# One diffusion-backbone layer on one Trainium2 core: the first adaLN product taken in blocks of output channels, inside the first projection

## The reference, cut to what matters

```python
mod_x = (silu(c) @ w_ada + b_ada)          # 6 x 1024 values
mod_c = (silu(c_ctx) @ w_ada + b_ada)
sh1, sc1, g1, sh2, sc2, g2 = split(mod_x, 6)
csh1, csc1, ... = split(mod_c, 6)
hc = rms(ctx) * norm_pre_mix * (1 + csc1) + csh1
hx = rms(x) * norm_pre_mix * (1 + sc1) + sh1
k_c, v_c = hc @ w_in[:, K_OFF:G_OFF]       # context: keys and values only
proj = hx @ w_in                           # q, k, v, gate, Fourier part
```

## Time and profile before

| | us |
|---|---|
| median of 3 runs (lowest, highest) | 1516.63 (1514.66, 1517.1) |
| the profiled execution, its time | 1513.78 |
| its span, first to last instruction | 1511.9 |
| TensorE busy (share of the span) | 1493.0 (99%) |
| VectorE, ScalarE, GpSimd busy | 1255.2, 588.9, 427.7 |
| first pass of the first projection starts | 42.60 |

### The profile page before, as it was taken

One profiled execution on the slowest core, in us unless ns is written; L12 is line 12 of the kernel. 1 busy time (PEld: TensorE's weight loads), 2 busy tenths in 40 slices (PEclk: granted clock), 3 DMA queues, 4 the chain that ended last, 5 costly groups with the idle time before them and its releaser, 6 DMA issues.

```text
span 1511.9 us, 21849 instructions
## 1 busy us (share of the span) xinstructions
PE 1493.0 (99%) x8129; PEld 1314.1 (87%) x8129; DVE 1255.2 (83%) x2378; ACT 588.9 (39%) x877; POOL 427.7 (28%) x365
## 2 busy tenths in 40 slices
PE   9999999999999999999999999999999999999998
PEld 4788888788999999999999999988888888888887
DVE  6888748766899997899999955688888888888886
ACT  6433133622233333444444443343333333333333
POOL 1020000000368888533222211321322222222210
PEclk9999999999999999999999999999999999999999
DMA  9685113134248887889999999999999999999983
GB/s 389 218 291 175 56 57 100 54 84 154 91 171 280 282 296 264 276 314 357 386 360 370 366 341 348 377 410 379 371 354 375 378 370 380 382 369 371 365 320 130
DMA packets 148438, 431.39 MB, mean 285 GB/s; under 512 B 13328, under 2 KB 46352, under 8 KB 145424
## 3 DMA queue, kind: packets, MB, share of 16 engines
q1 hardware_dynamic: 73152, 203.91, 37.0%
q0 software_dynamic: 41472, 151.01, 27.4%
q10 hardware_dynamic: 33744, 75.64, 13.2%
HBM read 375.98 MB, written 54.53 MB: 285 GB/s over the span
## 4 chain that ended last, share of the span: by engine, by line
PE 85%; DVE 10%; POOL 2%; DMA 1%; ACT 1%; issue 1%; ACTq 0%; SPq 0%; DVEq 0%
PE ps L1711 26%; PE ps L1713 25%; PE ps L1712 25%; PE ps L2122 3%; POOL ws_lo L610 1%; PE ps L2062 1%; DVE ps L1540 1%; DVE rows L1508 1%; DMA ada_w<-w_ada 1%; DVE ps L1544 1%; POOL rows L618 1%; DVE picks L1546 1%; PE ps L1956 0%; PE ps L1944 0%; DMA g_dram<-g_buf 0%
## 5 line engine op out<-in xcount | busy, mean ns | idle before, releaser
L1711 PE MATMUL ps<-hT_hi,ws_hi 128*128 128x384 f32 (+1 forms) x1184 | 412.0, 348 | 5.4 <-POOL ws_lo L610 4.3
L1713 PE MATMUL ps<-hT_hi,ws_lo 128*128 128x384 f32 (+1 forms) x1184 | 405.4, 342 | 0.0
L1712 PE MATMUL ps<-hT_lo,ws_hi 128*128 128x384 f32 (+1 forms) x1184 | 405.1, 342 | 0.0
L1711 PE MATMUL ps<-vs_hi,coef_hi 128*128 128x512 f32 x768 | 299.3, 390 | 1.1 <-DVE coef_lo L1670 1.1
L1712 PE MATMUL ps<-vs_lo,coef_hi 128*128 128x512 f32 x768 | 299.1, 389 | 0.0
L1713 PE MATMUL ps<-vs_hi,coef_lo 128*128 128x512 f32 x768 | 299.1, 389 | 0.0
L912 ACT ACTIVATE ws_hi<-blk_raw 128x1024 fp32r<-128x1024 f32 x128 | 135.7, 1060 | 323.2 <-PE ps L1713 323.2
L966 ACT ACTIVATE vs_hi<-blk_raw 128x1024 fp32r<-128x1024 f32 x128 | 135.7, 1060 | 285.3 <-PE ps L1713 282.8
L1711 PEld LDWEIGHTS ps<-hT_hi,ws_hi 128*128 128x128 f32 x1184 | 222.6, 188 | 14.8 <-issue 4.8
L1713 PEld LDWEIGHTS ps<-hT_hi,ws_lo 128*128 128x128 f32 x1184 | 222.3, 188 | 6.3
L1712 PEld LDWEIGHTS ps<-hT_lo,ws_hi 128*128 128x128 f32 x1184 | 222.7, 188 | 5.5
(11 more groups left out here) (321 smaller groups left out, 1850.7 us busy)
## 6 DMA issues: line engine op xcount, KB each, us to landing
blk_raw<-u_t SPq DMA_DIRECT2D x128, 512.0 KB, 6.1
blk_raw<-v_nat SPq DMA_DIRECT2D x128, 512.0 KB, 7.4
g_dram<-g_buf ACTq DMA_DIRECT2D x128, 192.0 KB
w_dram<-w_stage SPq DMA_DIRECT2D x48, 512.0 KB, 8.6
grp_g<-g_dram ACTq DMA_DIRECT2D x15, 1536.0 KB, 9.8
grp_w<-w_dram ACTq DMA_DIRECT2D x15, 1536.0 KB, 25.5
part_w<-w_ada POOLq DMA_DIRECT2D x32, 512.0 KB, 6.1
raw<-w_in SPq DMA_DIRECT2D x20, 512.0 KB, 6.4
```

What stands on the lines that cost most here:

```text
L1711: pe.matmul(o, lh, rh, start=start, stop=False, skip_group_check=True)
L1712: pe.matmul(o, lh, rl, start=False, stop=False, skip_group_check=True)
L1713: return pe.matmul(o, ll, rh, start=False, stop=stop, skip_group_check=True)
```

## The change

The host lays columns 0 to 2047 of w_ada out anew (ada_mix): block kc holds, for 128 output channels, all 1024 input rows of their shift and their scale, 1 MB. On the chip:

- ada_products(kc) takes the block's 2 x 8 tiles of 128 x 128 as weights in full precision and the two silu vectors as two moving columns. The sums come out as columns, in four spare columns of bank 7 (bank 5 for kc = 1); no splitting, no rows, no small transposes. modulation(kc) is two small VectorE steps per block.
- TensorE's order: block 0, x's transposes for kc = 0, then the projection's piece 0, in which kc's products of x and ctx stand beside the transposes of later channels and, after two of the four x products, the adaLN block kc + 1. VectorE modulates straight from PSUM; the copies to xT and cxT are gone.
- SyncE loads x in four pieces, then block 0, unit 0, ctx, and blocks and units by turns; before unit 8 it waits for all transposes of x. GpSimd's first part load waits for block 5's product, its third for the last transposes of ctx.
- x's squares start with each piece; the ctx norm moves behind block 0 on both engines. WARM is 9, KEEP is gone.

Lines of the same kind are cut; a line "..." stands for what is left out.

```diff
-ADA_WHOLE = 2
-ADA_HALVES = 2
-WARM = 12
-KEEP = 2
+WARM = 9
...
-        ada_w = [at(f"ada_w{k}", rE + 8 * K * k if k < 4 else rF + 8 * K * (k - 4), [2 * D]) for k in range(KC)]
...
+        ada_at = (rF, rF + 8 * K, rG, rG + 8 * K, rJ, rI + 8 * K, rI, rH)
+        ada_w = [at(f"ada_w{kc}", ada_at[kc], [KC, 2, P]) for kc in range(KC)]
+        junk_x = at("junk_x", rA + 12 * K, [D])
+        part_w = [at(f"part_w{i}", (rI + 8 * K, rI + 12 * K, rJ + 8 * K, rJ + 12 * K)[i], [D]) for i in range(PART_RING)]
...
+        ada_sums = [ps[:, 5 if kc == 1 else 7, NCTX:NCTX + 4].rearrange("p (s t) -> p s t", s=2) for kc in range(KC)]
...
+            def load_ada(kc):
+                sp.dma_start(ada_w[kc][:], ada_mix[kc:kc + 1, :, :].rearrange("a p n -> p (a n)")).then_inc(ada_in[kc], 16)
+
+            for tb in range(TB):
+                sp.dma_start(xs[:, tb, :], x[tb * P:(tb + 1) * P, :]).then_inc(x_in[tb], 16)
+            load_ada(0)
+            load_unit(0)
             sp.dma_start(cx[:], ctxt.rearrange("(b p) d -> p b d", p=P)).then_inc(cx_in, 16)
-            for kc in range(KC):
-                sp.dma_start(ada_w[kc][:], w_ada[kc * P:(kc + 1) * P, 0:2 * D]).then_inc(ada_in[kc], 16)
-            for n in range(n_units):
+            for j in range(1, RAW):
+                load_ada(2 * j - 1)
+                load_ada(2 * j)
+                load_unit(j)
+            load_ada(KC - 1)
+            for n in range(RAW, n_units):
                 if n == 8:
 
+                    sp.wait_ge(tr_done, KC)
...
-            pool.wait_ge(tr_done, 2 * KC)
+            pool.wait_ge(ada_used, 6)
             for u in range(parts):
+                if u == 2:
+
+                    pool.wait_ge(ctr_done, KC)
...
-            def take_x(kc):
...
             round_unit(0)
-            act.wait_ge(ada_used, KC)
-            act.activation(mod_rows[0:4, 0:D], ps[0:4, 0:2, :].rearrange("p a n -> p (a n)"),
-                           ACT.Copy).then_inc(rows_out, 1)
-            act.wait_ge(ada_done, 1)
-            act.activation(mod_rows[0:4, D:3 * 512], ps[0:4, 2, :], ACT.Copy).then_inc(rows_out, 1)
+            round_column(0, False)
+            act.wait_ge(cx_in, 16)
+            square(cx[:, 0, :], TB, 2)
+            act.wait_ge(ms_done, 5)
+            act.activation(rs[:, TB:TB + CB], ss[:, TB:TB + CB], ACT.Sqrt).then_inc(rt_done, 1)
+            for kc in range(KC):
+                round_column(kc, True)
+                if kc + 1 < KC:
+                    round_column(kc + 1, False)
+                if kc % 2 == 0 and kc < KC - 2:
+                    round_unit(kc // 2 + 1)
...
-            for kc in range(4):
...
+            def modulation(kc):
+
+                dve.wait_ge(ada_used, kc + 1)
+                dve.tensor_tensor(mod_b[:, kc::KC, :], ada_sums[kc],
+                                  colp[:, C_BADA + kc:C_BADA + 2 * KC:KC].unsqueeze(2).broadcast_to([P, 2, 2]),
+                                  ALU.add).then_inc(mod_step, 1)
+                dve.wait_ge(mod_step, 2 * kc + 1)
+                dve.tensor_scalar(mod_a[:, kc, :], mod_b[:, KC + kc, :], 1.0, colp[:, C_NPM + kc:C_NPM + kc + 1], ALU.add,
+                                  ALU.mult).then_inc(mod_step, 1)
+                dve.wait_ge(mod_step, 2 * kc + 2)
+
+            def modulated(kc, context):
+                t, src = ((xT, ps[:, 6, :]), (cxT, ps[:, 7, 0:NCTX]))[context]
+                dve.wait_ge((tr_done, ctr_done)[context], kc + 1)
+                dve.tensor_scalar(t[:, kc, :], src, mod_a[:, kc, context:context + 1], mod_b[:, kc, context:context + 1],
+                                  ALU.mult, ALU.add).then_inc(full_done, 1)
...
-            for j in range(4):
...
+            modulation(0)
+            modulated(0, 0)
+            rest_unit(0)
+            modulated_rest(0, 0)
+            dve.wait_ge(cx_in, 16)
+            square(cx[:, 1, :], TB + 1, 3)
+            scaled(1, cx, TB, CB, 3, 4)
+            for kc in range(KC):
+                modulated(kc, 1)
+                modulated_rest(kc, 1)
+                if kc + 1 < KC:
+                    modulation(kc + 1)
+                    modulated(kc + 1, 0)
+                    modulated_rest(kc + 1, 0)
+                if kc % 2 == 0 and kc < KC - 2:
+                    rest_unit(kc // 2 + 1)
...
+            def ada_products(kc):
 
                 pe.wait_ge(ada_in[kc], 16)
-                for n in range(4):
-                    last = pe.matmul(ps[0:4, n, :], csil[:, kc, :], ada_w[kc][:, n * 512:(n + 1) * 512],
-                                     start=kc == 0, stop=False, skip_group_check=True)
+                if kc >= 2:
+
+                    pe.wait_ge(full_done, 2 * kc)
+                for s in range(2):
+                    for k in range(KC):
+                        last = pe.matmul(ada_sums[kc][:, s, :], ada_w[kc][:, k, s, :], csil[:, k, 0:2], start=k == 0,
+                                         stop=k == KC - 1, skip_group_check=True)
                 last.then_inc(ada_used, 1)
 
-            def ada_split(kc):
...
+            def transposed(kc, context):
+                if kc:
+                    pe.wait_ge(full_done, 2 * kc - 1 + 2 * context)
+                else:
+                    pe.wait_ge(xn_done, (TB, TB + CB)[context])
+                for tb in range(CB if context else TB):
+                    src = (cx if context else xs)[:, tb, kc * P:(kc + 1) * P]
+                    last = pe.transpose(ps[:, 6 + context, tb * P:(tb + 1) * P], src, ident[:])
+                last.then_inc((tr_done, ctr_done)[context], 1)
 
             pe.wait_ge(iotas, 2)
             keep_busy(WARM)
             pe.wait_ge(silu_done, 1)
-            ada_chunk(0)
+            ada_products(0)
             pe.wait_ge(ident_ld, 16)
-            for kc in range(4):
...
+            transposed(0, 0)
...
+                    def row_product(kc, r):
+                        th, tl, tb, bank = rows_of[r]
+                        return split_mm(ps[:, bank, :], th[:, kc, tb * P:(tb + 1) * P], tl[:, kc, tb * P:(tb + 1) * P],
+                                        hi[:, kc % 2, :], lo[:, kc % 2, :], kc == 0, kc == KC - 1)
+
+                    for kc in range(2 * j, 2 * j + 2) if p == 0 else ():
+                        if kc:
+                            transposed(kc, 1)
+                            if kc + 1 < KC:
+                                transposed(kc + 1, 0)
+                        pe.wait_ge(full_lo, 2 * kc + 1)
+                        for r in range(TB):
+                            if kc and r == 2 and kc + 1 < KC:
+                                ada_products(kc + 1)
+                            row_product(kc, r)
+                        if kc == 0:
+                            transposed(1, 0)
+                            ada_products(1)
+                            transposed(0, 1)
+                        pe.wait_ge(full_lo, 2 * kc + 2)
+                        for r in range(TB, TB + CB):
+                            if kc == 0 and r == TB + 1:
+                                pe.wait_ge(mod_step, 3)
+                            last = row_product(kc, r)
...
+    ada_mix = ada[:, 0:2 * D].reshape(KC, P, 2, KC, P).transpose(3, 1, 0, 2, 4).reshape(KC, P, 2 * D)
```

More of the change, by code:

```diff
@@ L643, in _, with square @@
                            ACT.Silu).then_inc(silu_done, 1)
[L644 to L652, removed]
-            act.activation(guard[:], csil[:, 0, 2:3], ACT.Sqrt)
-            act.wait_ge(x_in, 16)
-            squares([(xs[:, tb, :], tb) for tb in range(2)], 0)
+            act.activation(guard[:], csil[:, 0, 2:3], ACT.Sqrt)
+            def square(src, bank, done):
+                if done:
+                    act.wait_ge(sq_done, done)
+                act.activation(junk[:], src, ACT.Square, accum_out=ss[:, bank:bank + 1]).then_inc(sq_done, 1)
+            act.wait_ge(x_in[0], 16)
+            square(xs[:, 0, :], 0, 0)
+            act.wait_ge(x_in[2], 16)
+            square(xs[:, 2, :], 2, 1)
             act.wait_ge(ms_done, 3)
             act.activation(rs[:, 0:TB], ss[:, 0:TB], ACT.Sqrt).then_inc(rt_done, 1)
[L659 to L662, removed]
             def round_full(src, dst, m):
@@ L738, in _ @@
                         take_piece(p - 1)
-                    if p or j:
+                    if p:
                         round_unit(4 * p + j)
[L741 to L745, removed]
                 if 0 < p < n_proj - 1:
@@ L1021, in _, with square, scaled @@
         def _(dve):
[L1022 to L1034, removed]
+            dve.wait_ge(silu_done, 1)
+            def square(src, bank, done):
+                if done:
+                    dve.wait_ge(ms_done, done)
+                dve.tensor_tensor_reduce(junk_x[:], src, src, 1.0, 0.0, ALU.mult, ALU.add,
+                                         ss[:, bank:bank + 1]).then_inc(ms_done, 1)
+            def scaled(i, t, first, count, by_act, by_dve):
+                dve.wait_ge(sq_done, by_act)
```

(13 more changed lines are left out.)

150 lines of the change are left out of this document (28 added, 122 removed).

## The result

The changed kernel takes **1548.92 us** (median of 4 runs, 1545.48 to 1550.22) where the kernel before, on the same chip, takes 1515.89: a ratio of 1.0211, 95% interval 1.0199 to 1.0224. It is slower by 33 us. The forecast was 1540, with a range of 1528 to 1554. The profiled execution took 1545.48 us, 31.7 more in its span than the earlier trace rows.

What follows compares the result with a forecast made beforehand. TensorE, busy 99% of the span, was taken as the bound, with VectorE's feed. Projection 9.8, piece 1 3.3 and turn() 7.9 make 21.0; clock 2.6 makes 23.6 on 1513.78, 1537.4; median 2.85 above: 1540 us, range 1528 to 1554.

Steps and rivals of the forecast that it cites:

- the list: First projection: TensorE's adaLN work goes from 18.3 to 29 us, so the projection ends at 85.1, 9.8 us later.
- the lead: VectorE's 8.1 us lead at piece 1 is lost: TensorE stalls 3.3 us there and 7.9 at turn().
- rival (b): First projection: each block's two-column passes drop the clock, slowing following products, 14 us more, 1552 us; chance 0.10.
- turn term: At turn() TensorE waits for VectorE's up_lo: 7.9 us, bounds 0 to 13.
- the start of piece 1: After the first projection: 9.8 us later from the projection plus a 3.3 us stall for rest_unit(4).
- I take 1.3 for each, 2.6: Clock lost after 2.8 idle us before the first products and 7 at turn(): 2.6 us together, bounds 0 and 8.
- 4.1 of 8.55 us are dense: First projection, argument against rival (b): 4.1 us of each 8.55 us kc are dense products.
- VectorE's stretch: From rest_unit(4)'s start to the end of up_lo, VectorE needs 68.8 us, as before the change.
- rival (a): Before turn(): VectorE catches up as part loads arrive without waits, turn() costs 0 to 3 us, 1533 us; chance 0.17.
- (c): adaLN blocks: two-column passes nearly free, 256 passes save 28 of 29 us, 1510 us; chance 0.04.
- (d): adaLN blocks: at 0.02 to 0.03 us a pass, gain and lost lead cancel, no change, 1516 us; chance 0.03.
- Rival (e): First projection: VectorE paces each kc, 1 us a kc, 7 us more, 1547 us; chance 0.08.

Runs made afterwards that it cites:

- Wide: Changed kernel with the silu columns repeated 64 times, so each adaLN pass streams 128 columns instead of 2; 1536.23 us, ratio 1.0143.
- reordered: Wide with only the order changed: unit 4's rest before VectorE's first three parts; 1538.69 us, one run.
- few-products: Wide with one instead of eight 128-row tiles in each adaLN sum of blocks 1 to 7; 1513.97 us, one run.
- Wide and parts together: Wide with eight of 32 parts added during the first projection and add_parts(0) taken from ahead of rest_unit(4); 1525.26 us, ratio 1.0065.
- interleaved kernel: Changed kernel with each block's 32 passes in four groups of eight, one behind each of x's products; 1555.04 us, ratio 1.0257.
- no-lead kernel: Kernel before the change, with VectorE held from unit 4's rest until TensorE is through with piece 0; 1525.73 us, ratio 1.0074.

## Why the prediction was right or wrong

**Right: direction, range, and the two terms of the list and of the lead.** The point was 9 us too low, and the range held the result because it had been stretched to rival (b), which had a chance of 0.10; a turn term 2 us too large hid a little of the miss. Wide tests the two terms without the clock of thin passes. First product 18.79 (18.5 forecast). Blocks 8.5 apart (8.55). Piece 0 over at 85.3 (85.1); the start of piece 1 moved by 12.9 (9.8 + 3.3 = 13.1); rest_unit(4) begun at 86.99 (87.15); turn() moved by 19.2, 135.18 to 154.39 (21.0). With 2.9 for the 14 products 0.43 apart behind turn() that makes 22.1, and its span is 21.8 above that of the earlier trace rows.

**The term that failed: "I take 1.3 for each, 2.6".** It charged the clock for idle time alone, and nothing for the thin passes between products. In the changed kernel:
- Piece 0: 96.41 against Wide's 85.29, **11.1 us**, for which the forecast had 1.3. It is rival (b), though not in every block (none of the products between blocks 2 and 3 ran slow): 3.7 up to block 3, 1.46 more in each of the next four kc (9.95 against Wide's 8.49), 5.8, and 1.6 in the last. The first products, too, run 0.43 apart, where Wide's, behind the same 2.8 us wait, run 0.23 apart: the thin block ahead of the wait had its part in it. Not all of it: in two later kernels with wide blocks (the reordered and the few-products one) the same wait was followed by some eight passes 0.43 apart, about 1.5 us, so the forecast's 1.3 for the wait can be right by itself, and how the 3.7 divide between wait and thin passes stays open.
- Start of piece 1: seven passes from 99.47 to 102.62, 3.15 where 1.59 would do, 1.6 us; as forecast, in VectorE's shadow, it only shortens the wait at turn().
- Behind turn(): 13 passes from 165.25 to 170.93, 5.68 for 2.95, **2.7 us**, for which the forecast had 1.3.

The sum as it came out: list 10.0, piece 1's wait and its start 3.0, clock in piece 0 11.1, the turn term 5.9, and 2.7 behind it, 32.7. sum_parts starts at 175.27 instead of 142.49, 32.8 later, and of these 31.7 are in the span. Rival (b)'s objection "4.1 of 8.55 us are dense" was no shield: the products that follow a block, nine in the kc shown, paid for it.

**The turn term, 7.9 forecast, 5.9 measured** (turn() 30.1 later, piece 1 24.1 later); 4.2 of it is the wait, 1.6 the slow start of piece 1 ahead of it. VectorE's stretch took 66.9 us, 98.19 to 165.10, and not 68.8, since it idled less before its parts. The group that answers to the earlier trace rows, in VectorE's groups of the changed kernel from 98.1 to 165.1 us:

```profile
L1070 DVE SCALAR_TENSOR_TENSOR part_acc<-part_w,csil,part_acc 128x1024 f32<-128x1024 f32 x26 | 33.4, 1284 | 7.9 <-DMA part_w<-w_ada 6.8
```

7.9 where it was 9.6: a step towards rival (a), no more.

**Rivals (c) and (d), nearly free passes,** fell with 0.108 a pass, which is what the row before had said. The few-products kernel says the same from the other side: 196 passes gone, and 0.11 us saved for each. Rival (e), VectorE pacing each kc, did not come: from block 3 on no wait of TensorE stands in the list.

**No version here with the whole product beats the kernel before.** The best, 1525.3, has next to no added wait from piece 1 on and no lost clock, and still carries the 10 us: the product with the activation as the moving operand loads 128 columns of weights for two useful ones, 29 us, where the other way round took 18.3. The earlier start could only repay that if TensorE had been idle before, and it had been working, on these same products, for most of that time.

## What to carry to other kernels

Count a small matrix-vector product on TensorE by its weight loads, not by its columns: with 128x128 weights a pass cost 0.11 us whether it streamed 2 columns or 128. And since the width was free, it should be used: the thin form cost a further 12.7 us, through the clock of the dense products behind it, while the wide form kept the clock and took 0.1 to 0.3 us more a block. Scattering the thin passes did not save the clock. Before work is moved, find how much lead each feeding engine has at the next rendezvous (here 8.1 us, all eaten 60 us later at turn()): a later start of its stretch costs what is beyond that lead, and a clock that must be won back on top.

## What the runs showed of the hardware that was not expected

- TensorE lost its full clock with no idle time at all. In the changed kernel 40 to 96 us are without a gap, and behind each of the five blocks that start from 44 us on, some eight matmuls run 0.43 apart: at once behind the first of these blocks, six products later behind the last. The products behind block 2 (36.13) ran at full clock. With 128 columns streamed instead of two the same stretch stays at 1.00.
- The thin run itself kept 2.4 GHz in those blocks, and the next products paid. The fall came with the first product at 47.82; in a later kc, after block 7 (84.13), six products still ran 0.23 apart, and the slow ones began at 89.12:

```profile
88.86 0.46 PE L1665 MATMUL ps<-ws_hi,hT_lo 128*128 128x512 f32 x1
89.12 0.63 PE L1663 MATMUL ps<-ws_hi,cT_hi 128*128 128x512 f32 x1
```

- A thin pass's price is a matter of the clock as well: eight took 0.95 at 2.4 GHz and, in the interleaved kernel, 1.70 at 1.2.
- Waits of equal length did not cost alike, not even with the same program up to there. Behind 2.80 us of waiting for hT_lo, at 18.79, Wide's products ran 0.23 apart throughout, and so they did in the kernel of Wide and parts together (18.84). In the reordered one (18.57) and the few-products one (18.06), which have the same instructions on TensorE up to that wait, some eight of them ran 0.43 apart. At piece 1, behind 2.82 us, Wide's fell to 0.43 from the third on, while behind 2.73 the few-products kernel's (67.12) kept 0.23. Behind 4.4 at Wide's turn() 14 ran 0.43 apart, behind 5.9 in the no-lead kernel eleven. What decides between these no run here tells apart.
